# A two-layer mixture-of-experts stage in a long f32 kernel: routing and experts in one block, tokens gathered four experts at a time

## The reference, cut to what matters

```python
def hierarchical_moe(x, w_group, b_group, w_expert, b_expert, w_gate, w_up, w_down):
    g_logits = t @ w_group + b_group                    # 4 groups
    g_sel = argmax(g_logits);  g_gate = max(softmax(g_logits))
    e_logits = (t @ w_expert + b_expert)[its group]     # 4 experts per group
    top_val, top_idx = lax.top_k(e_logits, 2)
    top_w = softmax(top_val) * g_gate                   # combine[:, e], 16 experts
    for e in range(N_EXPERTS):
        hid = silu(t @ w_gate[e]) * (t @ w_up[e])       # 1024 -> 512
        y = y + combine[:, e:e+1] * (hid @ w_down[e])   # 512 -> 1024
```

## Time and profile before

| | us |
|---|---|
| median of 3 runs | 2086.11 (2083.5 to 2087.96) |
| the profiled execution, its time | 2087.97 |
| its span, first to last instruction | 2086.2 |
| PE busy in the span | 1924.6 (92%) |
| DVE busy | 942.7 (45%) |
| ACT busy | 757.8 (36%) |
| DMA engines busy with the weight queue | 43.2% |

### The profile page before, as it was taken

How to read it: one execution, slowest core, us unless ns; L and a number is a source line. 1 busy time by engine, 2 the same in 40 slices (tenths; PEclk the granted TensorE clock), 3 DMA queues, 4 the chain that set the end, 5 groups by cost and what they waited for, 6 DMA issues and landing times. The chain is left out here.

```text
span 2086.2 us, 29645 instructions
## 1 busy us (share of the span) xinstructions
PE 1924.6 (92%) x12134; PEld 1401.3 (67%) x12134; DVE 942.7 (45%) x1836; ACT 757.8 (36%) x1434; POOL 0.2 (0%) x4
## 2 busy tenths in 40 slices
PE   7998999999996899998998998999978889999996
PEld 5777999766896789987877874333345787533332
DVE  6565655315676455655666562000034755410002
ACT  4454444114343344445554432212224444222221
POOL 0000000000000000000000000000000000000000
PEclk9999999999897999999999999999999999999999
DMA  6502443341001434424412330999952143069994
GB/s 277 202 36 87 182 182 147 118 171 67 22 3 39 183 129 190 170 109 152 178 65 101 122 145 9 422 427 427 424 207 82 36 182 146 4 257 427 426 429 191
DMA packets 24603, 374.04 MB, mean 179 GB/s; under 512 B 3856, under 2 KB 5008, under 8 KB 8096
## 3 DMA queue, kind: packets, MB, share of 16 engines
q1 hardware_dynamic: 21328, 363.89, 43.2%
q10 hardware_dynamic: 3152, 8.42, 1.3%
HBM read 371.25 MB, written 1.05 MB: 178 GB/s over the span
## 5 line engine op out<-in xcount | busy, mean ns | idle before, releaser
L1021 PE MATMUL ps<-ring,arena 128*64 128x512 f32 x1024 | 233.8, 598 | 0.0
L143 PE MATMUL ps<-ident 128*128 128x256 f32 x750 | 195.8, 407 | 36.2 <-PEq L485 7.5
L411 PE MATMUL ps<-ffn_x_h,ffn_w_h 128*128 128x256 f32 x704 | 202.5, 288 | 15.5 <-DVE ffn_w_l L406 15.5
L406 DVE TENSOR_TENSOR w_l<-ring,w_h 128x512 fp32r<-128x512 f32 x256 | 171.5, 690 | 84.3 <-ACT w_h L403 82.9
L403 ACT CAST w_h<-ring 128x512 fp32r<-128x512 f32 x256 | 156.2, 620 | 139.7 <-PE ps L411 139.1
L411 PE MATMUL ps<-ffn_x_h,ffn_w_l 128*128 128x256 f32 x704 | 202.2, 287 | 0.0
L411 PE MATMUL ps<-ffn_x_l,ffn_w_h 128*128 128x256 f32 x704 | 202.1, 287 | 0.0
L143 PEld LDWEIGHTS ps<-ident 128*128 128x128 f32 x750 | 145.1, 203 | 67.8 <-issue 49.0
L411 PE MATMUL ps<-w_h,x_h 128*128 128x512 f32 x416 | 163.8, 394 | 5.5 <-DVE w_l L406 5.5
L406 DVE TENSOR_TENSOR ffn_w_l<-ring,ffn_w_h 128x1024 fp32r<-128x1024 f32 x132 | 155.3, 1221 | 18.8 <-ACT ffn_w_h L403 18.8
L411 PE MATMUL ps<-w_h,x_l 128*128 128x512 f32 x416 | 162.0, 389 | 0.0
(11 more groups left out here) (333 smaller groups left out, 3061.9 us busy)
## 6 DMA issues: line engine op xcount, KB each, us to landing
ring<-in_w_moe SPq DMA_DIRECT2D x64, 3072.0 KB, 12.5
ring<-in_w_proj SPq DMA_DIRECT2D x38, 2048.0 KB, 8.7
ring<-in_w_ffn SPq DMA_DIRECT2D x22, 3072.0 KB, 10.1
rows<-in_ln_g ACTq DMA_DIRECT2D x6, 512.0 KB, 3.6
rows<-in_ln_b ACTq DMA_DIRECT2D x6, 512.0 KB, 5.2
ring<-in_w_lora SPq DMA_DIRECT2D x1, 2560.0 KB, 8.9
ring<-in_w_b_in SPq DMA_DIRECT2D x1, 2496.0 KB, 11.9
ring<-in_w_uq SPq DMA_DIRECT2D x1, 2048.0 KB, 8.6
```

The source lines that it names most:

```text
L143: pe.matmul(bank(b)[:, 0:2 * P].rearrange("p (o f) -> p o f", o=2), ident[:], wide, start=True, stop=True, skip_group_check=True)
L406: return dve.tensor_tensor(low, x, high.bitcast(F32), ALU.subtract)
L411: last = pe.matmul(out, a[x], b[y], start=start and n == 0, stop=stop and n == 2, skip_group_check=True)
L1021: mm = pe.matmul(bank(0)[own(k), :].rearrange("p (g n) -> p g n", g=2), xs[:, u // 2, k, :], w[:, :, k, :], start=(k < 2), stop=(k >= KD - ...
```

## The change

`experts` is gone and `mixture` holds both parts in one block.

- **Gather.** ACT casts `h` to fp32r (`token_h`), DVE takes the rest (`token_l`), both at the start of the block. Only the tokens of the first four experts are gathered before the units start: 8 k-tiles x 2 token tiles x 2 parts = 32 products of 256 columns in fp32r. The other twelve experts follow in `work_aside`, two k-tiles at a time, beside units 1, 2, 5 and 6 of each eight; the turned weights of two experts come beside units 0 and 4. `put` is written in two pieces, experts 0 to 3 first.
- **Branch.** DVE computes `overflow` before `place`. The sparse path stands first, unrolled over the 32 units, and the dense one behind it.
- **Clearing.** No products with zeros: the first scatter starts each bank.
- **Gate/up.** 16 products of 256 columns: gate goes to the lower 64 columns of the array, up to the upper 64, so that each half is complete. ACT takes the silu straight from PSUM, DVE multiplies by up, PE turns the product with two transposes, DVE copies it out.
- **Scatter** is per expert, not per two: the output of an expert is 64 tokens x 512 on each half of the partitions, and the four products have 64 rows each.
- **Ring.** The gate/up part of a slot is refilled when `gate_up` of its unit is done, the down part when `down` is, by two DMAs of 2048 and 1024 KB with semaphores of their own.
- **Scaling** of `h` by the previous norm's gain and bias (L242, L246) goes from the start of the experts into unit 9 on DVE.

```diff
+        def load_gate_up(sp, j):
+            sp.dma_start(ring[:, j % SLOTS, 0:DOWN_AT], loads[j][:, 0:DOWN_AT]).then_inc(loaded[j % SLOTS].up(16), 16)
+        def load_down(sp, j):
+            sp.dma_start(ring[:, j % SLOTS, DOWN_AT:UNIT], loads[j][:, DOWN_AT:UNIT]).then_inc(loaded_down[j % SLOTS].up(16), 16)
...
-                    fill(pe, 9)
+                    fill(pe, 6)
...
-                    fill(pe, 5)
...
-                            last = pe.matmul(bank(2 + n % 4), h[:, t, k * P:(k + 1) * P], put[:, t * D + c * half:t * D + (c + 1) * half], start=(t == 0), stop=(t == T - 1))
+                    fill(pe, 1)
...
+                        def gather(b, q, k, at):
+                            o = bank(b)[:, at * QUAD:(at + 1) * QUAD]
+                            for t in range(T):
+                                for x in range(2):
+                                    last = pe.matmul(o, parts_h[x][:, t, k * P:(k + 1) * P], put[:, t * D + q * QUAD:t * D + (q + 1) * QUAD],
...
+                            for k in range(KD):
...
+                                for g in range(2):
+                                    last = pe.matmul(bank(0)[g * SLOTS_E:(g + 1) * SLOTS_E, 0:2 * P], x[:, k, e * SLOTS_E:(e + 1) * SLOTS_E], wg[:, g, k, :],
...
+                        for n in range(EU):
+                            gate_up(n)
+                            if n % 2 and n >= 3:
+                                scatter((n - 3) // 2)
+                            if n:
+                                down(n - 1)
+                            work_aside(n)
+                            turn(n)
...
+                    for n in range(SLOTS, EU + 1):
+                        if n < EU:
+                            sp.wait_ge(gu.sem, gu.at(n - SLOTS + 1))
+                            load_gate_up(sp, j0 + n)
+                        if n > SLOTS:
+                            sp.wait_ge(dn.sem, dn.at(n - SLOTS))
+                            load_down(sp, j0 + n - 1)
```

More of the change, by code:

```diff
@@ new lines, in runs, with start, at @@
+                def runs(eng, body):
+                    for u in range(EPG):
+                        body(0, u, 1)
+                    with eng.Fori(1, steps - 1) as i:
+                        for u in range(EPG):
+                            body(i, u, steps - 2)
+                    for u in range(EPG):
+                        body(steps - 1, u, 1)
+                def start(i, n=0, u=0):
+                    return isinstance(i, int) and i == 0 and (n == 0 or u < n)
+                def at(i, u):
+                    return i * EPG + u
@@ new lines, in either, with scale @@
+                def either(eng, dense, sparse):
+                    eng.wait_ge(known.sem, known.at(1))
+                    counts = {s: s.count for s in signals.values()}
+                    full = eng.value_load(overflow[0:1, 0:1], min_val=0, max_val=1)
+                    with eng.If(full == 0):
+                        sparse()
+                    for s, n in counts.items():
+                        s.count = n
+                    with eng.Else():
+                        dense()
+                def scale(dve):
+                    unscaled[:] = scale_bias
+                    scale_rows(dve)
+                    dve.tensor_copy(stat[:, 40:41], stat[:, 36:37]).then_inc(scaled.up(), 1)
@@ L1891, in _ @@
+                    either(pe, dense, sparse)
                 @block.scalar
                 def _(act):
+                    for t in range(T):
+                        act.copy(parts_h[0][:, t, :], h[:, t, :]).then_inc(high.up(), 1)
                     act.wait_ge(e_in.sem, e_in.at(1))
@@ L1899, in _ @@
+                    either(act, dense, sparse)
                 @block.vector
@@ new lines, in _ @@
+                    either(dve, dense, sparse)
+                    for n, (t, c) in enumerate(QUARTERS):
+                        dve.wait_ge(summed.sem, summed.at(n + 1))
+                        add_residual(dve, t, c, ALPHA, bank(4 + 2 * t + c))
+                for n in range(EU):
+                    release[j0 + n] = dn.sem, dn.base + n + 1
+                last_load = min(j0 + EU + SLOTS, len(loads))
+                pos["issued"] = last_load
+                @block.sync
+                def _(sp):
+                    sp.dma_start(bias, d["route_b"][layer].rearrange("(o f) -> o f", o=1).broadcast_to([P, ROUTE])).then_inc(got.up(16), 16)
+                    sp.dma_start(w[:, 512:512 + 2 * P + SLOTS_E], d["slots"]).then_inc(got.up(16), 16)
+                    sp.dma_start(rank, d["rank"].rearrange("(o f) -> o f", o=1).broadcast_to([P, 4])).then_inc(got.up(16), 16)
+                    for n in range(SLOTS, EU + 1):
[5 more added lines that the diff above has]
+                            load_down(sp, j0 + n - 1)
+                    for j in range(j0 + EU, last_load):
+                        load(sp, j)
```

549 lines of the change are left out of this document (257 added, 292 removed).

## The result

The changed kernel takes 2009.55 us (median of four runs, 2005.62 to 2012.14) against 2085.9 us (four runs, 2083.5 to 2087.96): ratio 0.9633, 95% interval 0.9614 to 0.9652. Its profiled execution took 2012.14 us with a span of 2010.3, 75.9 less than the span before. The forecast was 2008 (2010.3 on the profiled execution's own time).

A forecast was written before the change was run, and what follows sets the result against it. PE was taken to pace the loop, DMA close behind, after 45 us without weight movement. Terms -78.7 + 1.6 - 0.6 = -77.7 from 2087.97 gave 2010.3, stated as 2008 us; range 1999 to 2042, with 2001 to 2017 at 0.60.

The forecast's parts named there:

- What bounds the kernel: Per mixture, 45 us in which no weight moves, then a loop where PE sets the pace, DMA at most 5% behind.
- Nothing grows in front of the places: Before the places: casts of `h` and the remainder run while PE makes the logits, so no time is added.
- A, the front: Stretch before the first unit: 45.64 and 45.49 us per mixture fall to 6.2, together -78.7 us.
- rival 4: Lower clock in gather and first unit, or an exposed branch: 4 to 7 us per mixture, 2019 us, chance 0.07.
- B, the loop: Loop over the units on PE: 234.2 us against 233.44, +0.8 per mixture, with handoffs hidden.
- C, the end: After the last down product: 7.6 us becomes 0.3 shorter per mixture, with PE's 4.1 us jump hidden.
- 1 (narrow products): Gate/up's 32 records start no closer than 0.12 us: 13.8 us more per mixture, 2036 us, chance 0.12.
- 2 (scatter halves): Scatter's products on the two row halves do not overlap: 27 us more per mixture, 2062 us, chance 0.07.
- 5 (instruction fetch): Unrolled loop: 26 fetches exposed at 4.1 us each, 2115 us, slower; chance 0.04 in full, 0.03 for a lesser share.
- 3 (DMA): Weight loads at 8.3 us per unit become the loop's bound, 12 us late per mixture: 2032 us, chance 0.07.

The follow-up runs named there:

- the last experiment: The kernel before the change with six fill products behind the counts instead of nine: 2083.63 us, ratio 0.998.

## Why the prediction was right, and where it was not

**What bounds the kernel:** right. The 45 us in which no weight moved are gone, and PE fills the loop in the changed kernel as well.

**Nothing grows in front of the places:** right, with a gain of 2.1 and 1.1 us that was not in the sum. By the last experiment it comes from the fills and the clock.

**A, the front:** the prediction counts from the first operation for the flag (1251.62), so its 6.2 answers to the 7.76 and 7.66 of the table. Flag and branch took nearly what was reckoned: the fills behind them begin at +1.41 (1253.03), where +1.25 stood. The terms that failed are the two that ran at the lower clock, the fills (1253.03 to 1254.53, 1.50 instead of 0.87) and the gather (1254.53 to 1259.38, 4.85 instead of 4.1):

```profile
1255.10 0.42 PE L1724 MATMUL ps<-places,token_l 128*128 128x256 f32 x1
...
1255.32 0.42 PE L1724 MATMUL ps<-places,token_h 128*128 128x256 f32 x1
...
1256.30 0.28 PE L1724 MATMUL ps<-places,token_l 128*128 128x256 f32 x1
...
1256.42 0.28 PE L1724 MATMUL ps<-places,token_h 128*128 128x256 f32 x1
```

Its first records start 0.22 us apart, the later ones 0.12 as in the earlier trace rows. The prediction had named this cost as a rival's and taken none of it, "since PE idles only about 1 us". That step was wrong: with 1.27 us of idle PE, behind small products that had already run at 0.69 to 0.83, the clock was at its lower level for the fills and the first products of the gather, and with more fills in front of the idle time it was not (1.00 over the whole front). It cost 1.4 per mixture, below the 4 to 7 of rival 4, since the products are back at full pace from 1256.2 on. The branch itself fell through, as hoped for: with the other order it costs 3.6 to 5.6, in the old kernel 6.8 with its effect on the clock. The rule of the Trainium skill (Runtime: NRT & Kernel Launch, Instruction fetch mechanics) on a taken branch agrees with both; it gives no time for it, and the runs do.

**B, the loop:** 231.41 us (1259.38 to 1490.79) where 234.2 stood. PE's timeline, one unit without and one with a scatter:

```profile
1330.29 3.67 PE L1738 MATMUL ps<-ring,arena 128*64 128x256 f32 x32
1333.79 1.89 PE L1759 MATMUL ps<-ring,routing 128*64 128x512 f32 x8
1335.61 0.39 PE L1724 MATMUL ps<-places,token_h 128*128 128x256 f32 x1
...
1336.76 0.34 PE L1790 MATMUL ps<-ident,arena 64*128 64x64 f32 x2
1337.03 3.67 PE L1738 MATMUL ps<-ring,arena 128*64 128x256 f32 x32
1340.63 1.99 PE L1748 MATMUL ps<-arena 64*128 64x512 f32 x8
1342.55 1.94 PE L1759 MATMUL ps<-ring,routing 128*64 128x512 f32 x8
1344.42 0.34 PE L1790 MATMUL ps<-ident,arena 64*128 64x64 f32 x2
1344.68 3.67 PE L1738 MATMUL ps<-ring,arena 128*64 128x256 f32 x32
...
1349.90 1.04 PE L1777 MATMUL ps<-ident,arena 128*64 128x128 f32 x16
1350.88 0.34 PE L1790 MATMUL ps<-ident,arena 64*128 64x64 f32 x2
```

Start to start: gate/up 3.50 and 3.60 (3.49 and 3.58 foretold), down 1.82 and behind a scatter 1.87 (1.82 foretold), scatter 1.92 (1.92 foretold). Mis-sized were the turn, 0.27 instead of 0.35 (32 x 0.08 = 2.6 us less), the turned weights, 0.98 instead of 1.2 (1.8 less), and the gather beside, 1.15 instead of 1.06 (1.1 more). The handoffs are hidden: no wait stands at any of these lines but at the last unit.

**C, the end:** from the copy of the last down product to the end of the last statistics 7.2 us (1490.79 to 1498.01) instead of 7.6: -0.4, foretold -0.3. PE's jump over the dense path is longer than the 4.1 us that were foretold. The branch instruction takes 6.37 us (its longest above; it starts at 1491.55, while the last scatter's products still run), and between that scatter and the next product PE is idle:

```profile
1498.44 3.65 PE L144 MATMUL ps<-ident 128*128 128x256 f32 x8 [4.94 <-PEq L1585]
```

The jump is over at 1497.92, DVE's last statistics at 1498.01, and the barrier takes both from there. Afterwards DVE waits 0.43 at the block's end, where it waited 0.38 before, so the jump is hidden but for that 0.05, with nothing to spare where the prediction gave it more than 1 us. The weight loads of the next stages fill the DMA engines in this stretch (share 1.01 from 1490.79 to 1498.01). At the end of the second mixture, with the engines at 0.02, the jump takes 3.55 us. DVE's own jump, for which 0.4 was allowed, takes 0.05.

**The rivals.** 1 (narrow products) is out by gate/up's 3.50, 2 (scatter halves) by 1.92 for eight records. 5 (instruction fetch) is out: DMA queues from 1300 to 1400 us,

```profile
q8 instruction: 6, 0.10, 0.4%
```

six fetches in the very window in which PE is busy for 100.00 us. 3 (DMA) did not come about, but its margin was thin. The prediction had the last weights landing at +222 and PE wanting them at +232. The last gate/up load is issued at 1457.06 and its loads take up to 16.5 us to land (the row below), so at +222 at the latest, as foretold; but PE, whose loop is shorter, asks for it at 1480.70, +229. Seven us, and the refill in one piece, whose stream is 6.6 us late at its start and 10.4 at its end, spends all of them. The prediction gave the two-part refill no term of its own; it is worth 3.2 per mixture, and my expectation for that experiment was wrong by the same omission. 4 (clock) came in part.

```profile
DMA to landing us min/median/max: 7.2/10.9/16.5
```

**The total was right partly by luck.** The mixtures gained 83.7 where 77.7 stood (choice 3.2, loop 5.7 and end 0.2 more; front 3.0 less). RWKV took 7.5 back in this execution. The windows of 20 us from 540 to 640 us, first and fourth, of before, then of after:

```profile
540.00:560.00 20.00, 18.62 (x482) 18.06 (x484) 6.73 (x17) 7.57 (x15) 0.00 (x0) 1.00 0.02 7
...
600.00:620.00 20.00, 20.00 (x480) 19.21 (x476) 16.35 (x26) 7.06 (x13) 0.00 (x0) 1.00 0.01 4
```

```profile
540.00:560.00 20.00, 18.87 (x460) 18.18 (x461) 6.36 (x15) 7.45 (x14) 0.00 (x0) 0.91 0.02 6
...
600.00:620.00 20.00, 20.00 (x444) 19.14 (x442) 15.40 (x24) 7.19 (x13) 0.00 (x0) 0.86 0.01 4
```

The same code, PE as busy, at a lower granted clock. In all three profiles of the old form RWKV took 99.7 us; in the nine of the new form 99.7 to 107.2, with the two of one and the same program at 107.2 and 101.2. Why is open: so few profiles do not separate chance from something in the program, and I tried nothing in that code.

## What to carry to other kernels

A block that gathers or routes everything before the first weight can move costs its whole length, and the DMA queue stands still for as long. Shorten it first: cheaper products, no clearing, no barrier, the turned weights beside the units and the right order of the paths took 26.4 us of the 45.6. Then put what the first units do not need beside the units, up to the point where PE takes as long per unit as the DMA (here 7.23 and 7.39 us); here that brought 3.8 more, since the units had almost no time to spare. Put the path that is taken first behind a branch, and keep PE at work up to the load that the branch needs: the jump cost about 4 us and the clock that fell after it up to 3 more. The jump then stands at the end of the block, so see to it that other work covers it there. Release a ring slot in the parts in which it is read when the stream has less slack than the time between the two releases.

## What the runs showed of the hardware

- PE's branch instruction takes 0.09 us when it falls through, and 3.3 to 4.0 us when it jumps over the other path at the start of a mixture. As idle time between products that is 3.8 to 3.9 us more (5.06 less 1.27; 5.36 less 1.47). At the end of a mixture, over the dense path, it takes 5.9 to 6.4 us in the first one, with the DMA engines full of weight loads, and 3.3 to 3.8 in the second, with the DMA engines all but idle (the eight kernels of the new form that have the sparse path first). DVE and ACT, with short paths, take 0.03 to 0.07 us either way.
- PE's clock goes to the lower level although PE never idles for long: 0.72 over a choice of experts with PE busy for 12.17 of 12.17 us with small products and fills. The same stage with the same number of fills took 12.17 us at a mean clock of 0.72 and 10.52 at 0.84.
- fp32r products of 256 columns with new weights each start 0.12 us apart at full clock and 0.21 to 0.22 at the lower one.
- Eight f32 records of 64 rows x 512 columns on alternating halves of the rows take 1.92 us, as four records over all rows did, and 32 records of 256 columns on alternating halves of the columns take 3.50 to 3.60, as 16 of 512 columns on the same halves did (3.49 to 3.58). So the halves overlap either way, down to 256 columns.
- Weights in one DMA of 24 KB per partition come at 420 GB/s with the engines at 1.01 (1303 to 1330 us of the kernel before), in two of 16 and 8 KB at 425 (1300 to 1400 us of the changed kernel).
- PE and DMA at full load do not slow each other measurably: a gate/up ahead of a scatter takes 3.60 us with the DMA engines at 1.01, and 3.60 for the last unit of the second mixture (1981.85 to 1985.45), where they stand at 0.00.
